# Inverse of the chunk matrices in a gated delta net: doubling levels on TensorE, or blocks solved on GpSimd and a series of products

## The reference

```
A = where(strict, beta * (k k^T) * decay, 0)          # per head and chunk
rhs = [v * beta, k * (beta * exp(G))]
sol = triangular_solve(eye + A, rhs, lower)           # u, w
u_new = u - w S ;  o = (q exp(G)) S + (q k^T * decay) u_new
S = S exp(G_last) + (k exp(G_last - G))^T u_new
```

## Time and profile before

| | us |
|---|---|
| median of 3 runs (lowest, highest) | 2937.09 (2936.52, 2937.82) |
| the profiled execution: its span from the first to the last instruction | 2936.8 |
| TensorE busy | 2862.6 |
| VectorE, ScalarE busy | 1725.2, 1342.0 |
| GpSimd busy | 141.7 |

### The profile page before, as it was taken

The page is one execution under the profiler, slowest core; times in us unless marked ns, Lnnn a source line. Parts: engine busy times, 40 slices in busy tenths (PEclk is TensorE's granted clock), DMA queues, the critical chain, the costliest instruction groups (busy, mean ns, idle before and its releaser), DMA issues.

```text
span 2936.8 us, 60061 instructions
## 1 busy us (share of the span) xinstructions
PE 2862.6 (97%) x22925; PEld 2803.5 (95%) x22925; DVE 1725.2 (59%) x3042; ACT 1342.0 (46%) x1999; POOL 141.7 (5%) x240
## 2 busy tenths in 40 slices
PE   6999999999999999999999999999999999999997
PEld 5999999999999999999999999999999999999997
DVE  5665565656566565655333555555677666776664
ACT  5434444444444443434334444334556544665563
POOL 2000000000000000000000000000011000100000
PEclk9999999999999999999899999999999999999998
DMA  6534343434333333437665555574799666995551
GB/s 208 169 98 126 107 127 110 125 105 121 111 117 118 111 112 119 123 117 217 182 197 171 175 172 172 172 261 145 223 315 294 209 207 188 317 300 183 174 169 63
DMA packets 435904, 494.13 MB, mean 168 GB/s; under 512 B 17329, under 2 KB 419498, under 8 KB 432866
## 3 DMA queue, kind: packets, MB, share of 16 engines
q1 hardware_dynamic: 415264, 415.42, 45.3%
q0 software_dynamic: 19872, 75.90, 8.2%
q10 hardware_dynamic: 578, 0.19, 0.0%
HBM read 467.67 MB, written 24.36 MB: 168 GB/s over the span
## 4 chain that ended last, share of the span: by engine, by line
PE 93%; DVE 3%; ACT 1%; issue 1%; DMA 0%; DVEq 0%; ACTq 0%
PE bank L579 93%; DVE wlo L1116 1%; ACT xhi L853 0%; DVE cacc L1272 0%; DVE GW L1255 0%; DMA vrow<-in_gdn_norm 0%; PE bank L627 0%; ACT whi L839 0%; DVE h L1534 0%; DVE xlo L1137 0%; ACT pp L993 0%; DVE hpro L1129 0%; DVE o_all L1260 0%; DVE cin L1333 0%; DVE xlo L1144 0%
## 5 line engine op out<-in xcount | busy, mean ns | idle before, releaser
L579 PE MATMUL bank<-xhi,whi 128*128 128x264 f32 x5520 | 1614.7, 293 | 43.2 <-issue 23.0
L579 PE MATMUL bank<-xlo,whi 128*128 128x264 f32 x5520 | 1584.1, 287 | 0.0
L579 PE MATMUL bank<-xhi,wlo 128*128 128x264 f32 x5520 | 1580.7, 286 | 0.0
L1116 DVE TENSOR_TENSOR wlo<-raw,whi 128x1024 fp32r<-128x1024 f32 x828 | 1007.8, 1224 | 799.2 <-ACT whi L839 797.2
L839 ACT ACTIVATE whi<-raw 128x1024 fp32r<-128x1024 f32 x828 | 874.4, 1059 | 788.7 <-PE bank L579 785.0
L579 PEld LDWEIGHTS bank<-xhi,whi 128*128 128x128 f32 x5520 | 1056.8, 191 | 61.0 <-issue 53.7
L579 PEld LDWEIGHTS bank<-xlo,whi 128*128 128x128 f32 x5520 | 1057.2, 192 | 4.5 <-issue 3.8
L579 PEld LDWEIGHTS bank<-xhi,wlo 128*128 128x128 f32 x5520 | 1054.8, 191 | 0.0
L579 PE MATMUL bank<-GW 128*128 128x128 f32 x2432 | 294.1, 275 | 0.0
L579 PEld LDWEIGHTS bank<-GW 128*128 128x128 f32 x2432 | 283.2, 192 | 0.0
L579 PE MATMUL bank<-ahi,wlo 128*128 128x264 f32 x704 | 200.1, 284 | 0.0
(11 more groups left out here) (259 smaller groups left out, 1655.6 us busy)
## 6 DMA issues: line engine op xcount, KB each, us to landing
raw<-in_w_in SPq DMA_DIRECT2D x356, 512.0 KB, 3.7
raw<-in_w_ffn_gate SPq DMA_DIRECT2D x88, 512.0 KB, 4.5
raw<-in_w_ffn_up SPq DMA_DIRECT2D x88, 512.0 KB, 4.8
raw<-in_w_ffn_down SPq DMA_DIRECT2D x96, 384.0 KB, 3.8
raw<-in_w_gdn_out SPq DMA_DIRECT2D x64, 512.0 KB, 3.5
chunkS<-in_state_gdn POOLq DMA_DIRECT2D x16, 1024.0 KB, 7.4
raw<-in_w_sconv_out SPq DMA_DIRECT2D x32, 512.0 KB, 3.6
raw<-in_w_o SPq DMA_DIRECT2D x32, 512.0 KB, 3.6
```

The source lines that it names most:

```text
L579: return pe.matmul(out, lhsT, rhs, start=start, stop=stop)
L1116: dve.tensor_tensor(wlo[:, at_ % SPLIT, :, :], raw[:, at_ % RAW, :, :], f32(whi[:, at_ % SPLIT, :, :]), ALU.subtract).then_inc(lo_ready, 1)
```

## The change

The inverse is no longer built by doubling. The negated matrix `N` (in `Tt`) is made as before, and beta moves from u to q k^T and to the scaled k. ScalarE issues DMAs that store the four 32x32 diagonal blocks of each of the 8 matrices in DRAM and, two pieces later, load them so that each partition holds one block for 8 of its 32 columns. GpSimd solves all of them by forward substitution: 31 times a product and a sum over what is left of the columns, each waiting for the one before. GpSimd stores the result and loads it as block diagonal tiles `DT`. TensorE then forms P^T = N D (masked by VectorE) and applies it to the right hand side: with t = D rhs, e = t + P t, f = P e, u = e + P f, that is (1 + P + P^2 + P^3) t, one product per step and head, separately for each chunk.

The order of the pairs becomes q, k, v0, v1, z, sc, sh, z, and a group starts in the turn in which its q, k and v are computed ("cur") and ends in the next ("prev"). All of the first group's pairs stand in `first` (36 pieces), and `last_group` has 24 pieces. The levels' masks go, new tiles come, and the ring of raw weights shrinks from 8 to 4 buffers. `DT`, the number of row tiles, is renamed `DTL`.

```diff
-RAW = 8
+RAW = 4
...
+SB = 32
+QC = 8
...
-        QKVS = ("v0", "v1", "q", "k")
+        def layer_pairs(gx):
+            return [qkvpair(k, gx) for k in ("q", "k", "v0", "v1")] + [zpair(0, gx), spair("sc", SC0, gx), spair("sh", SH0, gx), zpair(1, gx)]
+
         phases = [
-            Phase("first", 1, [mk(win, lambda it: A0, X, "ab", tiles=1, xr="attn")] + [qkvpair(k, const(0)) for k in QKVS] + [zpair(p, const(0)) for p in range(2)]),
-            Phase("groups", NG - 1, [spair("sc", SC0, cur), spair("sh", SH0, cur), qkvpair("v0", nxt), qkvpair("v1", nxt),
-                                     zpair(0, nxt), qkvpair("q", nxt), qkvpair("k", nxt), zpair(1, nxt)]),
-            Phase("last_group", 1, [spair("sc", SC0, const(NG - 1)), spair("sh", SH0, const(NG - 1))]
-                  + [spair("sb", SB0, const(i)) for i in range(6)]),
+            Phase("first", 1, [mk(win, lambda it: A0, X, "ab", tiles=1, xr="attn")] + layer_pairs(const(0))),
+            Phase("groups", NG - 1, layer_pairs(nxt)),
+            Phase("last_group", 1, [spair("sb", SB0, const(i)) for i in range(6)]),
...
-        LEVELS = {p: (p - 3,) for p in range(8, 20)}
-        PE_STEP = {0: (0,), 1: ("decay",), 2: (1,), 5: (3,), 7: (4,), **LEVELS, 20: (17, 23), 21: (18,), 22: (19,), 23: (20,),
-                   24: (21,), 26: (22,)}
-        ACT_STEP = {0: (0,), 3: (1,), 4: (2,), 5: (3,), 7: (4,), **LEVELS, 21: (23, 18), 24: (21,), 27: (22,)}
-        DVE_STEP = {0: ("decay",), 2: ("exponents",), 4: (2,), 5: (3,), 7: (4,), **LEVELS, 20: (17,), 22: (19,), 23: (20,),
-                    24: (21,), 29: (23,)}
+        PE_STEP = {"cur": {9: ("decay",), 10: ("sums",), 12: ("kkqk",), 14: ("nturn",), 18: ("tails",), 19: ("vturn",), 26: ("pt",),
+                           27: ("pt0",), 28: ("pe0",), 29: ("pf0",), 30: ("s1",), 31: ("ks",)},
+                   "prev": {0: ("t1",), 1: ("pt1",), 2: ("pe1",), 3: ("pf1",), 4: ("o1",), 5: ("osum",), 6: ("sct",)}}
+        ACT_STEP = {"cur": {10: ("squares",), 11: ("root", "exps"), 13: ("kcopy",), 14: ("blk_store",), 15: ("ncopy",), 16: ("blk_load",),
+                            19: ("stage",), 20: ("vcopy",), 26: ("t0c",), 28: ("f0c",), 30: ("s1c",)},
+                    "prev": {0: ("t1c",), 2: ("f1c",), 4: ("osq",), 5: ("oroot",), 7: ("sct",)}}
+        DVE_STEP = {"cur": {9: ("gsel",), 10: ("exponents",), 12: ("qkn",), 13: ("lt",), 26: ("mask",), 27: ("e0",), 28: ("ktok",),
+                            29: ("u0",), 31: ("r",)},
+                    "prev": {1: ("e1",), 3: ("u1",), 4: ("s2",), 7: ("o",)}}
...
+            def solve(grp):
+
+                pool.wait_ge(g["blk_in"], grp * 64 + 64)
+                pool.sem_inc(pool_passed, 1)
+                mine.inc(pool.tensor_copy(sol[:, :, :], unit[:, :, :]))
+                for j in range(SB - 1):
+                    n = SB - 1 - j
+                    mine.settle(pool)
+                    mine.inc(pool.tensor_tensor(prod[:, :, 0:n], blk[:, j, j + 1:SB].unsqueeze(1).to_broadcast([P, QC, n]),
+                                                sol[:, :, j:j + 1].to_broadcast([P, QC, n]), ALU.mult))
+                    mine.settle(pool)
+                    mine.inc(pool.tensor_tensor(sol[:, :, j + 1:SB], sol[:, :, j + 1:SB], prod[:, :, 0:n], ALU.add))
+                mine.settle(pool)
+                pool.sem_inc(g["solved"], 1)
+
+            def solution_out(grp):
+
+                pool.wait_ge(g["solved"], grp + 1)
+                pool.sem_inc(pool_passed, 1)
+                for q in range(4):
+                    pool.dma_start(sol_d[:, :, QC * q:QC * q + QC, :].rearrange("m b c i -> (m b) (c i)"),
+                                   sol[SB * q:SB * q + SB, :, :].rearrange("p c i -> p (c i)")).then_inc(g["sol_stored"], 16)
+                pool.wait_ge(g["sol_stored"], grp * 64 + 64)
+                pool.sem_inc(pool_passed, 1)
+                for b in range(4):
+                    pool.dma_start(DT[SB * b:SB * b + SB, :, SB * b:SB * b + SB],
+                                   sol_d[:, b, :, :].rearrange("m c i -> c m i")).then_inc(g["dt_in"], 16)
...
+            def group(grp, first, last):
+                load_state(grp, 2)
+                load_state(grp, 3)
+                pool.wait_ge(sc_turned, grp + 1)
+                pool.sem_inc(pool_passed, 1)
+                pool.dma_start(st_sc[:, :, :], sts[:, ds(grp * COLS, COLS)].rearrange("r (t p) -> r t p", p=P)).then_inc(sc_in, 16)
+                if not first:
+                    finish(grp - 1)
+                if not last:
+                    load_state(grp + 1, 0)
+                    load_state(grp + 1, 1)
+                solve(grp)
+                solution_out(grp)
+                tails_out(grp)
...
-                elif 5 <= slot <= 16 and slot % 2:
-                    lv = (slot - 5) // 2 + 1
-                    pe.wait_ge(g["x"], LV * gr + lv)
+                elif slot == "pt":
+                    pe.wait_ge(tails_staged, gr + 1)
+                    pe.wait_ge(g["vcopied"], gr + 1)
+                    pe.wait_ge(g["dt_in"], gr * 64 + 64)
                     for c in range(NCH):
-                        for i in range(4):
-                            s = slice(i * CH, i * CH + CH)
-                            m = mm(B[4 + c][:, s], GW[:, 5 * c + 1, s], GW[:, 5 * c + 3, s])
-                    m.then_inc(g["y"], 1)
-                elif 5 <= slot <= 16:
-                    lv = (slot - 6) // 2 + 1
-                    pe.wait_ge(g["ycopied"], (LV - 1) * gr + lv)
-                    for c in range(NCH):
-                        for i in range(4):
-                            s = slice(i * CH, i * CH + CH)
-                            if lv < LV - 1:
-                                mm(B[4 + c][:, s], GW[:, 5 * c + 4, s], GW[:, 5 * c, s])
-                            m = mm(B[6 + c][:, s], GW[:, 5 * c, s], GW[:, 5 * c + 4, s])
-                    m.then_inc(g["xy"], 1)
-                elif slot == 17:
-                    pe.wait_ge(g["x"], LV * gr + LV)
-                    for i in range(4):
-                        s = slice(i * CH, i * CH + CH)
-                        m = mm(B[4][:, s], GW[:, 4, s], vTok[:, 0, i, :])
-                    m.then_inc(g["u0"], 1)
-                elif slot == 18:
-                    pe.wait_ge(g["u0s"], gr + 1)
-                    for i in range(4):
-                        s = slice(i * CH, i * CH + CH)
-                        mm(B[5][:, s], GW[:, 3, s], GW[:, 1, s])
-                        m = mm(B[6][:, s], GW[:, 1, s], GW[:, 2, s])
+                        for i, s in enumerate(heads):
+                            m = mm(B[4 + c][:, s], Nn[:, c, s], DT[:, 4 * c + i, :])
+                    m.then_inc(g["pt"], 1)
+                    for i, s in enumerate(heads):
+                        m = mm(B[6][:, s], DT[:, i, :], vTok[:, 0, i, :])
+                    m.then_inc(g["t0"], 1)
+                elif slot == "pt0":
+                    pe.wait_ge(g["masked"], gr + 1)
+                    pe.wait_ge(g["t0c"], gr + 1)
+                    apply(B[7], E, 0).then_inc(g["pt0"], 1)
+                elif slot == "pe0":
+                    pe.wait_ge(g["e0"], gr + 1)
+                    apply(B[6], Tt, 0).then_inc(g["pe0"], 1)
+                elif slot == "pf0":
+                    pe.wait_ge(g["f0c"], gr + 1)
+                    apply(B[7], E, 0).then_inc(g["pf0"], 1)
...
+                elif slot == "blk_store":
+                    act.wait_ge(g["lt"], gr + 1)
+                    for b in range(4):
+                        act.dma_start(blk_d[:, b, :, :].rearrange("m j i -> j m i"),
+                                      Tt[SB * b:SB * b + SB, :, :].rearrange("p c (i t) -> p (c i) t", i=4)[:, :, SB * b:SB * b + SB]
+                                      ).then_inc(g["blk_stored"], 16)
...
+                elif slot == "blk_load":
+                    act.wait_ge(g["blk_stored"], gr * 64 + 64)
+                    for q in range(4):
+                        act.dma_start(blk[SB * q:SB * q + SB, :, :].rearrange("p j i -> p (j i)"),
+                                      blk_d.rearrange("m b j i -> (m b) (j i)")).then_inc(g["blk_in"], 16)
...
+                elif slot in ("t0c", "f0c"):
+                    act.wait_ge(g[{"t0c": "t0", "f0c": "pe0"}[slot]], gr + 1)
+                    act.activation(E[:, 0, :], bank[6][:, :], ACT.Copy).then_inc(g[slot], 1)
...
+                elif slot == "mask":
+                    dve.wait_ge(g["pt"], gr + 1)
                     for c in range(NCH):
-                        dve.copy_predicated(H4(5 * c + 4), M(joinT, 0), H4(5 * c + 1))
-                    dve.wait_ge(g["lt_turned"], gr + 1)
-                    dve.sem_inc(dve_passed, 1)
+                        m = dve.tensor_tensor(H4(PT, c), bank[4 + c][:, :].rearrange("p (a b) -> p a b", a=4),
+                                              below[:, :].unsqueeze(1).to_broadcast([P, 4, CH]), ALU.mult)
```

(34 more changed lines are left out.)

509 lines of the change are left out of this document (244 added, 265 removed).

## The result

The kernel after takes 3087.23 us (median; 3085.48 to 3090.03), the one before 2937.45 us on the same chip: a ratio of 1.0498 (95% interval 1.048 to 1.0516). The change makes the kernel 150 us slower. The forecast was 3014, slower, with a range of 2880 to 3100.

What follows compares the result with a forecast made beforehand. TensorE, busy 97%, was taken to bound the kernel: 2936.8 - 181 (products) + 142 (wait at pt) + 60 (decay) + 38 (qkn) + 18 (clock) = 3014 us, range 2880 to 3100.

Steps and rivals of the forecast that it cites:

- the wait at pt: TensorE waits before pt for the solve's result: 17.7 us a group, 142 us over eight.
- the two waits from the order: TensorE waits for VectorE behind convolutions: decay selection 8.6 us, 60 in all; qkn 4.8 us, 38 in all.
- A: The forecast itself: solve outlasts its window, waits eat the 181 us; 3014 us, own range 2945 to 3070, chance 0.40.
- B: Rival: GpSimd stands still in VectorE's splits, solve 12 us longer; +96, 3110 us, chance 0.25.
- the clock: TensorE runs slow after idling, added once per group for the wait at pt: 18 us (0 to 50).
- Products removed: TensorE issues 208 fewer instructions a group at 0.109 us: 22.7 us a group, 181 us saved over eight.
- The window of the solve: From the end of kkqk: GpSimd starts at 16.6 us, TensorE comes to pt at 46.2.
- The solve: GpSimd's copy and 62 dependent operations per group: 37 us, low end 18, high end 43 without contention.
- B's sign: In the new profile, a GpSimd operation would take a VectorE split's length more when they meet.
- Stores and loads of the solution: Four stores and four loads after the solve, before pt: 10.2 us a group.
- The ring: Raw weight buffers cut from 8 to 4: nothing in groups, 0 taken in the FFN, upper end 20 us.
- D: Rival: the shorter ring of raw weights starves the FFN; +20 us, 3034 us, chance 0.05.

Runs made afterwards that it cites:

- short splits: Kernel after with VectorE's weight splits in slots 17 to 26 cut to one of four k tiles, output not the reference's; 3023.5 us.
- columns in turn: Kernel after with each solve's eight columns taken in turn, so step j works on only j//4 + 1 of them (elements 7936 -> 3120); 3022.0 us.
- vector order: Kernel after with VectorE's decay selection in slot 6, ScalarE's root of o in slot 6 and o in VectorE slot 8; 3003.5 us.
- kkqk one slot later: Kernel after with kkqk, kcopy, lt, nturn, block store, ncopy and block load one slot (2.9 us) later; 3056.4 us.
- products in the wait: Kernel after with 140 never-read products on TensorE ahead of the wait for DT before pt; 3088.5 us.
- the version at 2915.0: Kernel after with vector order, columns in turn, earlier unit copy, pt and later steps two slots later, block load in slot 15; ratio 0.9906 to before.
- gsel in slot 6: Kernel after with VectorE's selection for the decay rows in slot 6 in place of 9; 3033.4 us.
- three slots later: The version at 2915.0 with pt and later steps shifted three slots in place of two, gsel in slot 7, o in slot 10; 2949.3 us.
- sct moved: The version three slots later with sct in slot 8 on TensorE and ScalarE, no longer directly ahead of the decay step; 2959.5 us.

## Why the prediction was right, and where its sizes were off

The sign and the mechanism were right: the wait at pt and the two waits from the order are there and eat what the products gave. The time lies 73 us above the forecast, outside A's own range (2945 to 3070) and nearer to B's 3110. Two things were mis-sized or left out of the sum: the clock (18 us for 66 of busy time, ring included) and the stops of GpSimd in VectorE's splits (nothing in the sum, 8 to 9 us a group measured), and the second is hidden by an error the other way.

**Products removed: right.** 208 a group fewer, 181 us. No run isolates it; it fits the account below.

**The window of the solve: right to within 1 us.** From the end of kkqk and its turns (620.7) to GpSimd's start 15.9 us (16.6 forecast), and to TensorE's arrival at pt 45.8 (46.2).

**The solve: 37 us forecast, 41.7 measured, and for another reason.** Less hindered it is shorter than I said: 33 us with the short splits (27.6 + 4.9 of gaps + 0.5), since the gap between dependent instructions is 0.08 us, not 0.15. What I gave to rival B, in which GpSimd stands still in VectorE's splits, is real and adds 8 to 9 us a group (I had priced it at 12). So A's number was nearly met by luck, with an error in each direction, and B's mechanism holds: an instruction that meets a split of 1.23 us takes 0.93 us longer, three quarters of what I had named as B's sign. The Trainium skill (SBUF — State Buffer, "Who interferes with whom") says that a VectorE instruction with two SBUF inputs and a GpSimd one that reads SBUF exclude each other for the whole instruction. On GpSimd's side the runs agree in the main: such an instruction does more than half of its work behind the split. I should have put B's price into the sum rather than beside it. By that section whoever starts first keeps the port. The split at 624.09 in the run with the columns in turn would be the other direction: it starts 0.01 us after a GpSimd sum of 0.31 us and takes 1.39 us for 1.23, so 0.16 longer, about half of that sum. A stop of VectorE for the whole GpSimd instruction is thus not shown; what there is stays small (the splits' mean is 1.231 us after, 1.224 before).

**Stores and loads of the solution: 10.2 forecast, 7.8 measured.** They landed in 1.8 and 1.6 us (679.02 to 686.85). Wait at pt: 15.9 + 41.7 + 0.7 + 7.8 - 45.8 = 20.3 us, 162 in all for 142.

**The two waits from the order: right.** Decay 53 us for 60, kkqk 39 for 38. In the kernel after VectorE comes to both steps from a convolution and the splits behind it (to the selection at 593.56 from that of k, to qkn at 613.87 from that of v0), as counted. The run with the vector order shows that the first goes when VectorE has its steps in another order.

**The clock: the term that failed.** I said: "I add it once per group, for the wait at pt: 18 us", and that behind the decay wait the slower pieces "only shorten the qkn wait". They do not: that wait is 38.6 us with the decay step at half clock (kernel after) and 38.6 with it at full clock (vector order). TensorE's busy time came to 2747.2 where 2862.6 - 181 = 2681.6 was due: 66 us more. All three waits bring half clock: the decay step takes 3.78 us for 1.98, kkqk 3.79 for 2.05, its turns 1.06 for 0.60, pt 3.53 for 2.05. That is 1.8 x 7 + (1.7 + 0.5 + 1.5) x 8 = 42 us. The short ring has 10.6 in the run that has only that. The rest, some 13, are weight pieces behind the waits: the one behind the decay step takes 4.26 us (765.66 to 769.92) where one at full clock takes 2.95, the two behind kkqk's turn 6.54 (620.30 to 626.84) for 5.91 with kkqk one slot later (606.14 to 612.05), so 1.3 x 7 + 0.6 x 8 = 14 us. Not all of it is time won when it goes: with products in the wait pt was faster in half of the groups, and the time stayed.

**The ring: 0 forecast, 20 as the upper end, 23 measured** for it alone. It was right for the groups and wrong for the start and for what comes behind them, where I had read one landing (12.7 us) and called it covered. D's price of 20 was right, its place only in part: 7 us fall at the start. No run gives the kernel after its eight buffers back, so that the ring costs the same there is assumed.

**The account.** 2936.8 - 181 + 162 + 53 + 39 + 66 (busy) + 11 (other idle) = 3087 us, for a span of 3086.7. Of the 73 us between forecast and result the clock and the ring's busy time are 48, the wait at pt 20, other idle 11, the order waits -6. The sign and the mechanism stand: the solve on the slow engine outlasts its window, and the waits eat what the products gave. Without the solve the same kernel takes 2904.7 us, and with the columns in turn, another vector order and pt two slots later 2915.0.

Open: what the version at 2915.0 gains from kkqk one slot later, which was worth 31 us in the kernel after; what its loads of the solution wait for; and why the same wait leaves TensorE at full clock in one group and at half in the next.

## What to carry to other kernels

Work moved off the busiest engine pays only if its latency, with the handshakes at both ends, fits the window that this engine can fill; add up the window, then everything that can stop the other engine inside it, splits of a neighbour included. A wait on a saturated TensorE can be paid twice, when the clock drops in it, so price every such wait with the step and the piece behind it at half speed, and ask of a wait of 5 us whether a piece can be put before it. When a wait is moved, look for the next engine behind it: in three of the runs here (gsel in slot 6, three slots later, sct moved) part or all of it came back under another name. And read more than one group: in two of the runs some groups ran a step at full clock and some at half, which one group's timeline doesn't tell.

## What the runs showed of the hardware

- A GpSimd product or sum of fp32 tiles with two SBUF inputs, which meets no split, takes 0.21 us for 8 elements per partition and 0.61 (product) to 0.71 (sum) for 248 (kkqk one slot later, first solve instructions at 621.65 and 622.33), with 0.08 us between dependent ones: 1.7 to 2.0 ns per element.
- A GpSimd instruction that starts in a 1.23 us VectorE split with two SBUF inputs ends about 0.4 us after it with 192 to 208 elements per partition, and 0.17 us after it with 68 to 76 (columns in turn): that is more than half of the 0.54 to 0.60 us and of the 0.31 us that such an instruction takes alone.
- The last wait's length alone does not set the clock. Behind waits of 4.9, 7.4 and 20.4 us it was 0.50 in the kernel after. Behind the same wait of 3.3 us (products in the wait) it was 1.00 in four groups and 0.50 in the other four, in turn; behind the same wait of 1.94 us (kkqk one slot later) the next step took 2.05 us in four groups and 3.5 to 3.6 in four. And in the kernel after the window behind a wait of 1.7 us at the loop's edge (715 to 720 us) shows 0.77, between windows of 0.89 and 1.00.
